# HGRN and GLA attention in a fused two-block model: values multiplied by chunks of 64 tokens on row halves, even and odd chunks in a bank each

## The reference, cut to what matters

```python
scores = jnp.einsum('bhnck,bhnsk->bhncs', qe, ke)
scores = jnp.where(causal, scores, 0.0)              # 64 x 64 within a chunk
o_intra = jnp.einsum('bhncs,bhnsv->bhncv', scores, v)
...
o_inter = jnp.einsum('bhnck,nbhkv->bhncv', qe, S_prev)
o = o_intra + o_inter
...
o = o * lax.rsqrt(jnp.mean(o * o, axis=-1, keepdims=True) + EPS) * norm_w
o = o.reshape(B, T, D_HG) * jax.nn.silu(gf)
```

## Time and profile before

| | |
|---|---|
| median of 3 runs | 2295.97 us |
| the profiled execution, its time | 2294.73 us |
| its span | 2293.0 us |
| mean granted TensorE clock | 0.993 |
| busy: PE / PEld / DVE / ACT / POOL | 98% / 79% / 46% / 27% / 50% |
| HBM traffic | 101 GB/s over the span |

### The profile page before, as it was taken

The page is one execution under the profiler, slowest core; times in us unless marked ns, Lnnn a source line. Parts: engine busy times, 40 slices in busy tenths (PEclk is TensorE's granted clock), DMA queues, the critical chain, the costliest instruction groups (busy, mean ns, idle before and its releaser), DMA issues.

```text
span 2293.0 us, 29768 instructions
## 1 busy us (share of the span) xinstructions
PE 2241.7 (98%) x11352; PEld 1814.7 (79%) x11352; DVE 1055.7 (46%) x1196; ACT 616.9 (27%) x712; POOL 1147.1 (50%) x1106
## 2 busy tenths in 40 slices
PE   8999999999999999999999999999999999999996
PEld 5788887787788787778888788777888888888885
DVE  7888772356633251441686146456432101223306
ACT  6543342335432231121133232243211000111111
POOL 3332224666543232232663343666666676666675
PEclk9999999999999999999999999999999999999998
DMA  6234422232421111111112334424322333323343
GB/s 231 74 117 180 152 92 81 85 99 83 155 75 37 56 56 65 47 54 58 38 65 73 106 124 153 159 92 156 101 96 96 101 102 101 99 95 97 118 158 119
DMA packets 68760, 231.95 MB, mean 101 GB/s; under 512 B 7344, under 2 KB 8512, under 8 KB 68672
## 3 DMA queue, kind: packets, MB, share of 16 engines
q1 hardware_dynamic: 65216, 218.15, 28.4%
q10 hardware_dynamic: 3456, 12.58, 1.4%
HBM read 205.54 MB, written 25.17 MB: 101 GB/s over the span
## 4 chain that ended last, share of the span: by engine, by line
PE 88%; DVE 4%; issue 3%; ACT 2%; POOL 1%; DVEq 1%; POOLq 0%; DMA 0%; ACTq 0%; SPq 0%
PE PG L597 41%; PE PG L638 17%; PE PG L684 15%; PE PG L1063 5%; POOL WL L517 1%; PE PG L1075 1%; PE PX L789 1%; PE PX L713 1%; PE PX L784 1%; DVE WK L1726 1%; PE PX L795 1%; PE PX L767 0%; DVE PX L1732 0%; POOLq L516 0%; PE PX L928 0%
## 5 line engine op out<-in xcount | busy, mean ns | idle before, releaser
L517 POOL TENSOR_TENSOR WL<-WRAW,WH 128x1024 fp32r<-128x1024 f32 (+2 forms) x304 | 704.5, 2317 | 45.1 <-issue 0.9
L514 POOL TENSOR_TENSOR TOUCH<-TOUCH 128x2 f32<-128x2 f32 x304 | 84.3, 277 | 1063.5 <-PE PG L684 353.3
L597 PE MATMUL PG<-UL,WH 128*128 128x512 f32 x1072 | 417.9, 390 | 0.0
L597 PE MATMUL PG<-UH,WH 128*128 128x512 f32 x960 | 377.3, 393 | 3.4 <-DVE H L2078 2.4
L597 PE MATMUL PG<-UH,WL 128*128 128x512 f32 x960 | 374.2, 390 | 0.0
L515 POOL TENSOR_SCALAR WH<-WRAW 128x1024 fp32r<-128x1024 f32 (+2 forms) x304 | 309.3, 1017 | 0.0
L597 PEld LDWEIGHTS PG<-UL,WH 128*128 128x128 f32 x1072 | 201.6, 188 | 43.1 <-issue 1.9
L638 PE MATMUL PG<-UH,WH 128*128 128x512 f32 x576 | 226.4, 393 | 2.8 <-DVE WK L1836 1.2
L638 PE MATMUL PG<-UH,WL 128*128 128x512 f32 x576 | 224.2, 389 | 0.0
L638 PE MATMUL PG<-UL,WH 128*128 128x512 f32 x576 | 224.1, 389 | 0.0
L684 PE MATMUL PG<-UH,WH 128*128 128x512 f32 x544 | 222.8, 410 | 0.0
(11 more groups left out here) (493 smaller groups left out, 3471.3 us busy)
## 6 DMA issues: line engine op xcount, KB each, us to landing
WRAW<-up_w SPq DMA_DIRECT2D x88, 512.0 KB, 3.5
ADA<-ada_w SPq DMA_DIRECT2D x24, 1024.0 KB, 5.4
WRAW<-down_w SPq DMA_DIRECT2D x48, 512.0 KB, 3.5
WRAW<-out_w SPq DMA_DIRECT2D x30, 512.0 KB, 3.6
WRAW<-zg_w SPq DMA_DIRECT2D x24, 512.0 KB, 3.4
gates<-STG ACTq DMA_DIRECT2D x24, 512.0 KB, 2.6
WK<-gates SPq DMA_DIRECT2D x24, 512.0 KB, 3.4
WRAW<-gla_w SPq DMA_DIRECT2D x18, 512.0 KB, 3.5
```

The costliest lines, as they stand in the source:

```text
L514: pool.tensor_tensor(TOUCH[:, 0:2], TOUCH[:, 2:4], TOUCH[:, 4:6], ALU.add)
L517: pool.tensor_tensor(WL[:, r, 0:n], WRAW[:, r, 0:n], WH[:, r, 0:n].bitcast(F32), ALU.subtract).then_inc(w_split, 1)
L597: mm = pe.matmul(PG[:, bank, :], w[:, r, P * k:P * k + P], v, start=first and k == 0 and n == 0, stop=last and k == kbs - 1 and n == 2)
```

## The change

A value matmul takes one chunk of 64 tokens instead of 128 tokens: the stationary operand is 64 token rows by 128 value columns, the moving one 64 rows by the 64 score columns of the same chunk. Chunks alternate between the row halves 0 to 63 and 64 to 127. Even chunks of the whole sequence go to bank 0, odd ones to bank 1, both in the value and in the state matmuls. Whoever reads the output reads the two banks in turns: the Square in one instruction through a rearranged view, the scaling by the norm weight in one instruction per bank. Order of the steps, fillers, plans, semaphores and buffers stay.

```diff
+    def by_chunk(x):
+
+        return x.rearrange("p (t c q) -> p t c q", c=2, q=CH)
+
+    LA_OUT = PX[:, 0:2, :].rearrange("p c (t q) -> p t c q", q=CH)
...
                         for t in range(4 * half, 4 * half + 4):
-                            pe.matmul(PX[:, half, P * (t % 4):P * (t % 4) + P], WK[:, vt[hh], P * t:P * t + P],
-                                      WK[:, att[hh], P * t:P * t + P], start=t % 4 == 0, stop=False)
+                            for c in range(2):
+                                tok = slice(CH * c, CH * c + CH)
+                                pe.matmul(PX[:, c, CH * t:CH * t + CH], WK[tok, vt[hh], P * t:P * t + P],
+                                          WK[tok, att[hh], P * t + CH * c:P * t + CH * c + CH],
+                                          start=t == 0, stop=False)
                         for n in range(8 * half, 8 * half + 8):
-                            at = CH * (n % 8)
+                            at = CH * (n // 2)
                             for v in range(0, P, 64):
-                                mm = pe.matmul(PX[v:v + 64, half, at:at + CH], states[:, P * n + v:P * n + v + 64],
-                                               WK[rows, qe0, CH * n:CH * n + CH], start=False, stop=n % 8 == 7)
+                                mm = pe.matmul(PX[v:v + 64, n % 2, at:at + CH], states[:, P * n + v:P * n + v + 64],
+                                               WK[rows, qe0, CH * n:CH * n + CH], start=False, stop=n >= 14)
...
-                    act.activation(WK[:, sqo, :], aux(0), ACT.Square).then_inc(la["sq"], 1)
+                    act.activation(by_chunk(WK[:, sqo, :]), LA_OUT, ACT.Square).then_inc(la["sq"], 1)
...
-                dve.scalar_tensor_tensor(WK[:, 6, :], aux(0), vec("hg_norm_w"), WK[:, 6, :], ALU.mult, ALU.mult)
+                for c in range(2):
+                    y = by_chunk(WK[:, 6, :])[:, :, c]
+                    dve.scalar_tensor_tensor(y, LA_OUT[:, :, c], vec("hg_norm_w"), y, ALU.mult, ALU.mult)
...
-                    dve.scalar_tensor_tensor(WK[:, 3, :], aux(0), vec_at("gla_norm_w", i * 2 + hh), WK[:, 2, :],
-                                             ALU.mult, ALU.mult)
+                    for c in range(2):
+                        dve.scalar_tensor_tensor(by_chunk(WK[:, 3, :])[:, :, c], LA_OUT[:, :, c],
+                                                 vec_at("gla_norm_w", i * 2 + hh), by_chunk(WK[:, 2, :])[:, :, c],
+                                                 ALU.mult, ALU.mult)
```

## The result

The changed kernel is slower, by a third of a per cent: 2303.61 us median of 18 runs against 2296.41 for the kernel before, a ratio of 1.0033 with a 95% interval of 1.0026 to 1.0040. Forecast was 2298.7 in a range of 2291.2 to 2302.0, with "within 0.2%" as the likeliest outcome. The measured time lies above the range and outside the likeliest outcome, while most of the predicted steps came out in the trace. I take those first.

A forecast was written before the change was run, and what follows sets the result against it. TensorE, busy 98% of the 2293.0 us span, was taken as the bound. 2.0 + 0.06 us on PE and 0.66 from DVE gave +2.7 us, 2298.7 against a median of 2295.97, range 2291.2 to 2302.0.

The forecast's parts named there:

- Counts and tiles: In 16 output halves, value matmuls go from 8 to 16 instructions each, keeping 128 stationary columns; state matmuls keep their number.
- The step is the load's: In the value matmuls, the 128-column weight load sets 0.058 us per instruction, so a half's value part takes 1.10 us.
- entry: On PE, going from a full-array weight product to row-half value matmuls loses 0.08 us.
- A half after a product: The 10 attention halves following a weight product each cost 0.20 us more on PE, +2.0 us together.
- PE's own sum: Attention halves on PE: +2.0 us for 10 after a product and +0.06 for the other 6.
- DVE and ACT: Norm scaling split in two costs +0.22 us a head, exposed at two GLA waits and last HGRN result: +0.66; ACT 0.
- The Square: ACT's 1.03 us instruction, reading two banks in turns, stays hidden up to 1.7 us more; taken as 0.
- The sum at full clock: Whole kernel: 2.0 + 0.06 on PE and 0.66 from DVE, +2.7 us, with no term for the clock.
- The step that failed: Whole kernel: attention time added to or taken off PE reaches the end one for one, unless PE then waits.
- 1: Value matmuls: the load does not bind, step falls to 0.030 us, -4.0 us in all, 2292.0; chance 0.13.
- 2: Value matmuls: full doubling, each value part costs half, entries nothing, -7.5 us in all, 2288.5; chance 0.06.
- Rival 3: Array empties between row-half value matmuls and state tiles, 0.3 us more 16 times, +7.5 us in all, 2303.5; chance 0.11.

The follow-up runs named there:

- e4: Changed kernel with value matmuls on all 128 rows for each chunk's 64 moving columns, no row halves; 2314.07 us in its one run.
- e3: Changed kernel with HGRN's value matmuls cut into quadrants, 64x64 stationary, GLA left as changed; ratio 1.0011 to the kernel before.
- e9: Kernel before with weight products moved from between the first GLA head's halves to behind its sum; 2298.65 us, ratio 1.0011.
- e12: Kernel before with HGRN values in 64x64 quadrants, plus weight products moved behind the first GLA head's sum; 2297.79 us, ratio 1.0009.
- e18: Changed kernel with weight products moved from between the first GLA head's halves to behind its sum; ratio 1.0009 to the kernel before.
- e6: The change made in the two GLA pairs alone, HGRN as in the kernel before; ratio 1.0012 to the kernel before.
- e15: Changed kernel with 2.25 us of idle multiplication ahead of the last GLA head's sum; 2306.06 us, ratio 1.0036 to the kernel before.
- e2: Changed kernel with the norm-weight scaling in one DVE instruction over both banks instead of two; ratio 1.0020 to the kernel before.
- e13: Kernel before with 1.1 us of idle multiplication ahead of the last GLA head's sum; ratio 1.0012.
- e17: The changed kernel unaltered, run again beside its variant with covered waits; ratio 1.0039 to the kernel before.
- e11: The changed kernel unaltered, run again on the same chip as two plan variants; ratio 1.0030 to the kernel before.

## Why the prediction was wrong

- **Counts and tiles**: right (256 L792 instructions, 187 ns loads of 128 columns).
- **The step is the load's**: right, and shown by e4 and e3. Forecast 1.10 us a value part, measured 1.04; entry forecast 0.08, measured 0.09. A half after a product costs 0.15 more and not 0.20, for an HGRN head 0.10 in all; a GLA half after a wait takes 0.05 less (1.04 against 1.09). PE's own sum is about 1.2 us instead of 2.06.
- **DVE and ACT**: the places were right, the second GLA heads and, by little, the output product. The sizes were 0.12 and 0.47 at the GLA heads and 0.1 at the output product instead of 0.22 each, the 0.47 with 0.42 us of issue in it. That the three add up to 0.7, near the 0.66 of the forecast, is luck. The Square was right at 0.
- **The sum at full clock**: +2.7 forecast, +1.9 measured over all runs.
- **The step that failed** stands in the first part: "A microsecond that this attention takes off PE's instruction stream, or adds, therefore reaches the end one for one, provided that PE does not then wait". I priced a longer wait at its own length, and the clock was taken as given for the whole kernel from its nine tenths in every slice. A slice is 57 us, and a stretch of 3.4 us at half clock takes only 0.03 off it. What the runs showed in its place: 1.9 us more at full clock came with about 5.4 us more lost to the clock, so that the time grew by 7.3. The trace before held the warning, behind the wait of 3.1 us in PE's timeline:

```profile
361.35 0.80 PE L660 MATMUL PG<-UH,WH 128*128 128x512 f32 x1 [3.09 <-DVE UL L1967]
...
362.37 0.63 PE L660 MATMUL PG<-UH,WL 128*128 128x512 f32 x1
362.80 0.63 PE L660 MATMUL PG<-UH,WH 128*128 128x512 f32 x1
```

The output product runs at 0.43 us a step there, half clock. The sum has no term for the clock and gives no reason for leaving it out; measured it is about 5.4 us, twice the whole forecast. Longer waits at the second GLA heads are shown to have a part in it, by the stretches near 695 and 805 us; how large a part stays open.
- **Rivals**: 1 and 2 fell with the value part of 1.04 us, and e4 shows why. Rival 3 had the right side and by chance the right size (2303.5), but not the mechanism: L798 starts 0.21 us after L792's last start (184.66 against 183.62 + 1.11 - 0.28), as long as L789 behind L784 in the kernel before.

**Open**: what lets the clock fall between 860 and 945 us; why e9 and e12, with the second heads' waits covered, lose 3 us more to the clock than before, and e18 does not; why e6 and e15, with long waits, lose less than the changed kernel; whether row halves have a share of their own beside the waits (e2 loses 2.3 more, no different from the 2.4 of e13, which has no new row halves); and what the 0.42 us of issue are. A wait of PE on POOL's L523 of about 1 us near 1603 us comes and goes between kernels and was not followed up.

## What to carry to other kernels

Row halves gained nothing here with 128 stationary and 64 moving columns, while quadrants of 64x64 did: compare the weight load with the moving side before counting on a factor of two, and cut the stationary columns if the load is the longer. Price a wait of TensorE not only by its length but also by what the clock may do behind it, and when a small change makes the time move several times its own cost, take the runs apart by span x clock and span x (1 - clock), and look first at what part of the half-clock time lies where TensorE has nothing left to do. One profile of each kernel can show a convincing pattern of clock stretches that a dozen runs do not have.

## What was not expected of the hardware

- Waits of 0.87 and 1.22 us, with ordinary work on both sides, were followed by stretches of 3.4 us at 1.2 GHz in some executions of the same kernel (e17: 6.8 us at a stretch from 803.7) and by none in others (e11).
- Quadrants of 64x64 ran 32 fp32 instructions in 0.62 us, at a step of 0.015 us, four tiles side by side.
- Two DVE instructions of 128x512 in a row took 1.41 us, less than twice 0.746; an ACT read that changes the PSUM bank every 64 elements cost the same 1.027 us as a straight one.
